# Loads of the first token tiles reordered, norm gains on ScalarE's queue, and two unused products ahead of the first turns, in a hybrid attention and DeltaNet layer

## The reference, cut to what matters

```
hn = _rms_norm(h, norm_gain)
proj = hn @ w_in                      # 1024 -> 3020 columns
(c_q, c_kv, k_idx, w_idx, z_attn, q_g, k_g, v_g, z_g, b_g, a_g) = _split_last(proj, IN_PROJ_SPLITS)
o_attn = _dsa_mixer(c_q, c_kv, k_idx, w_idx, ...) * silu(z_attn)
o_gdn = _gdn_mixer(q_g, k_g, v_g, z_g, b_g, a_g, ...)
y = concatenate([o_attn, o_gdn]) @ w_out
return h + y
```

## Time and profile before

| what | value |
|---|---|
| median of 3 runs | 849.3 us (847.48 to 850.51) |
| profiled execution, its own time | 850.14 us |
| its span, first to last instruction | 848.4 us |
| TensorE busy | 810.3 us, 96% |
| VectorE busy | 605.5 us, 71% |
| ScalarE busy | 390.3 us, 46% |
| GpSimd busy | 252.0 us, 30% |
| mean granted TensorE clock | 0.982 of full |

### The profile page before, as it was taken

The page is one execution under the profiler, slowest core; times in us unless marked ns, Lnnn a source line. Parts: engine busy times, 40 slices in busy tenths (PEclk is TensorE's granted clock), DMA queues, the critical chain, the costliest instruction groups (busy, mean ns, idle before and its releaser), DMA issues.

```text
span 848.4 us, 16491 instructions
## 1 busy us (share of the span) xinstructions
PE 810.3 (96%) x6345; PEld 486.9 (57%) x6345; DVE 605.5 (71%) x1405; ACT 390.3 (46%) x1218; POOL 252.0 (30%) x254
## 2 busy tenths in 40 slices
PE   6999999999999999999969999999899999999998
PEld 2555434444445666666636667766676566566564
DVE  2353789999999999999866667667656665575541
ACT  3444767776692545555445445575421222132111
POOL 8000100000000545467744522355323232332310
PEclk9999999999999999999979999999969999999999
DMA  6262200013003002000100021203221320222011
GB/s 163 83 214 98 77 13 26 25 41 130 30 13 124 0 1 99 1 0 1 46 29 2 25 100 33 85 26 115 95 99 59 101 96 12 96 77 76 27 51 50
DMA packets 29507, 51.72 MB, mean 61 GB/s; under 512 B 3684, under 2 KB 11220, under 8 KB 29428
## 3 DMA queue, kind: packets, MB, share of 16 engines
q1 hardware_dynamic: 28884, 50.55, 17.7%
q0 software_dynamic: 544, 0.10, 0.4%
HBM read 40.11 MB, written 12.10 MB: 62 GB/s over the span
## 4 chain that ended last, share of the span: by engine, by line
PE 87%; DVE 6%; ACT 3%; issue 3%; DMA 1%; POOL 0%; DVEq 0%; ACTq 0%; POOLq 0%
PE ps L1683 20%; PE ps L1661 12%; PE ps L1894 11%; PE ps L1538 7%; PE ps L1732 5%; PE ps L1721 5%; PE ps L1703 4%; PE ps L1795 2%; PE ps L1635 2%; PE ps L1815 2%; PE ps L1856 1%; PE ps L1589 1%; PE ps L1831 1%; PE ps L1870 1%; PE ps L1633 1%
## 5 line engine op out<-in xcount | busy, mean ns | idle before, releaser
L1200 DVE TENSOR_SCALAR_CACHE_REDUCE junk<-scores,iw 128x272 bf16<-128x272 f32 (+6 forms) x224 | 213.6, 954 | 8.2
L1683 PE MATMUL ps<-areaH,areaW 128*128 128x384 f32 (+1 forms) x576 | 168.1, 455 | 1.6 <-ACT areaQ L936 1.6
L1683 PEld LDWEIGHTS ps<-areaH,areaW 128*128 128x128 f32 x576 | 109.4, 190 | 59.9 <-issue 1.8
L748 POOL TENSOR_TENSOR staging<-staging,areaC 128x520 f32<-128x520 f32 x60 | 88.1, 1502 | 63.9 <-ACT areaC L974 63.9
L762 POOL TENSOR_TENSOR areaH<-areaQ,masks 128x512 f32<-128x512 f32 x37 | 45.3, 1229 | 90.1 <-PE ps L1815 82.2
L795 POOL TENSOR_TENSOR areaW<-scores,tmp 128x256 f32<-128x256 f32 (+1 forms) x64 | 45.0, 727 | 62.4 <-DVE small L1286 53.1
L1538 PE MATMUL ps<-areaW,areaH 128*128 128x460 f32 (+1 forms) x144 | 59.9, 571 | 2.0 <-DVE areaH L1122 1.9
L1894 PE MATMUL ps<-areaW,scores 128*128 128x512 f32 x128 | 59.2, 604 | 0.0
L974 ACT ACTIVATE areaC<-areaC,small 128x520 f32<-128x520 f32 x60 | 42.6, 726 | 33.9 <-POOL staging L748 33.9
L1661 PE MATMUL ps<-areaH,areaW 128*128 128x512 f32 x128 | 56.5, 594 | 0.0
L1661 PE MATMUL ps<-areaW,areaH 128*128 128x512 f32 x128 | 56.2, 592 | 0.0
(11 more groups left out here) (272 smaller groups left out, 1439.8 us busy)
## 6 DMA issues: line engine op xcount, KB each, us to landing
areaW<-in_w_in SPq DMA_DIRECT2D x5, 2048.0 KB, 8.0
areaH<-row_factor_scratch SPq DMA_DIRECT2D x18, 256.0 KB, 4.5
areaC<-in_x SPq DMA_DIRECT2D x8, 512.0 KB, 3.6
tmp<-in_x SPq DMA_DIRECT2D x8, 512.0 KB, 5.0
y<-tmp SPq DMA_DIRECT2D x7, 512.0 KB, 3.3
areaW<-in_w_out SPq DMA_DIRECT2D x3, 768.0 KB, 6.6
gate_a_scratch<-staging SPq DMA_DIRECT2D x8, 256.0 KB, 2.3
gate_g_scratch<-staging SPq DMA_DIRECT2D x8, 256.0 KB, 2.0
```

Source lines behind the costliest of these rows:

```text
L748: nc.gpsimd.tensor_tensor(sums, sums, prod, ALU.add).then_inc(s_cvP, 1)
L1200: tlink(V.tensor_scalar(junk[:, 0:n], scores[:, SC0[i]:SC0[i] + n], at, init, op, ALU.add, accum_out=cnt[:, i - 1:i]))
L1683: ins = mm(ps[:, n % 4, 0:hi - lo], wslot[:, g % 2, k, 128 * m:128 * m + 128], hT[:, k, lo:hi], start=k == 0, stop=k == KD - 1)
```

## The change

Three edits at the start of the program:

1. SP waits until the last of the first weights (`w_first7`) has landed before it asks for tiles 2 to 8. Tile 2 was asked for directly behind the issue of those weights.
2. The three loads of gains (`norm_gain` as 128x8 single values, `cq_norm_gain` as 128x2, `ckv_norm_gain` as 128x1) go out from ScalarE's queue, ahead of its table load, and no longer from POOL's.
3. VectorE clears 512 columns of `areaQ` as its third constant (the clearing of `junk` becomes its fourth), and TensorE multiplies that with itself twice into bank 7, a 128x128 by 128x512 f32 product each, ahead of its wait for the identity matrix. Nothing reads the result.

```
-        N_CONST, N_DCONST, N_PAR = 22, 3, 16 * 12
+        N_CONST, N_DCONST, N_PAR = 22, 4, 16 * 12
...
                 if k == 3:
                     load_x(1)
+            sp.wait_ge(s_wk[KD - 1], 16)
             for t in range(2, NT):
                 load_x(t)
...
         @block.gpsimd
         def _(pool):
             par = [
-                (gain, norm_gain[0].rearrange("(k p) -> p k", p=128)),
-                (gc[:, 0:2], g_cq[0].rearrange("(k p) -> p k", p=128)),
-                (gc[:, 2:3], g_ckv[0].rearrange("(k p) -> p k", p=128)),
...
-            for dst, src in par[0:3]:
-                pool.dma_start(dst, src).then_inc(s_gain, 16)
...
-            for dst, src in par[3:]:
+            for dst, src in par:
                 pool.dma_start(dst, src).then_inc(s_par, 16)
...
+            act.dma_start(gain, norm_gain[0].rearrange("(k p) -> p k", p=128)).then_inc(s_gain, 16)
+            act.dma_start(gc[:, 0:2], g_cq[0].rearrange("(k p) -> p k", p=128)).then_inc(s_gain, 16)
+            act.dma_start(gc[:, 2:3], g_ckv[0].rearrange("(k p) -> p k", p=128)).then_inc(s_gain, 16)
             nc.scalar.preload_act_table_set("natural_log_exp_and_others")
             act.wait_ge(s_dconst, N_DCONST)
...
             dlink(V.memset(ba, 0.0))
+            dlink(V.memset(areaQ[:, 0:512], 0.0))
             dlink(V.memset(junk[:, :], 0.0))
...
             mm, turn = nc.tensor.matmul, nc.tensor.transpose
+            pe.wait_ge(s_dconst, 3)
+            for _ in range(2):
+                mm(ps[:, 7, :], areaQ[:, 0:128], areaQ[:, 0:512], start=True, stop=True)
             pe.wait_ge(s_const, 3)
```

## The result

The changed kernel is slower: median 856.4 us of 8 runs (850.56 to 858.12) against 848.39 of 8 runs of the kernel before (845.77 to 850.51) beside them; the ratio is 1.0079, with a 95% interval of 1.0058 to 1.0101. The prediction said 852.7, slower. Its direction was right; its size, +3.4 us, is half of the +6.7 that the ratio gives.

What follows compares the result with a forecast made beforehand. TensorE, busy 96% of the span, was taken as the bound, with projection 1's start deciding. Terms +1.6 + 0.5 + 1.3 + 0 + 0 = +3.4 us on 849.3 gave 852.7 us, range 849.2 to 855.0.

Steps and rivals of the forecast that it cites:

- The number to watch: Start of projection 1 on TensorE, 19.67 us before the change; whatever moves it was to move the rest of the kernel.
- Two chains that end together: Before projection 1, TensorE's own chain and tile 2's arrive at 18.3 within 0.1 us; speeding projection 0 alone gives next to nothing.
- Part 1: SP's wait: weights land at 13.4, tile 2 at 17.3 instead of 15.7; +1.6 us, ends +0.8 and +3.2.
- Part 2: Gains on ScalarE's queue: projection 0 starts near 7.5 instead of 8.61, 1.1 us gained but hidden behind tile 2's chain.
- Part 3: The two products on TensorE, done by 5.3 before turn 0, delay nothing; worth 0 on the path.
- The clock: TensorE idles 4.8 us before turn 2, so its clock falls: +0.5 us in turn 2, +1.3 in projection 1.
- B: Weights land at about 11.8 without tile 2 beside them, cancelling its lateness: -1 to +0.8 us; chance 0.15.
- C: Weights' stream brakes both chains: `w_first7` lands by about 9.3, projection 1 starts at 17.2, -2.5 us; chance 0.08.
- A: Tile 2 is late but TensorE's clock holds or falls briefly: +0.8 to +2.5 us; chance 0.27, shared with another rival.

Runs made afterwards that it cites:

- no_wait: The changed kernel without SP's wait, gains on ScalarE's queue and the two products kept; ratio 1.0050 to the kernel before.
- gains_only: The kernel before with only the gains' loads moved to ScalarE's queue, so POOL's twelve small loads start at 2.10 us instead of 4.97; ratio 1.0068.
- products_only: The kernel before with only the two unused products and the clearing they read; ratio 1.0003.
- wait_only: The kernel before with only SP's wait for the last first weights; ratio 1.0032.
- small_loads_last: The kernel before with POOL's twelve small loads moved behind its last constant and the landing of the last first weights; ratio 0.9998.
- changed_again: The changed kernel unaltered, profiled a second time; 855.92 us, span 854.2.
- broadcast_last: The kernel before with gains on ScalarE's queue and, of POOL's small loads, only that of `gdn_norm_gain` moved behind the last first weights; ratio 1.0036.

## Why the prediction was wrong where it was, point by point

**The number to watch** was nearly right. In eleven kernels beside the one before the time followed the end of projection 1, nearly within what the timing can tell. The start alone is not enough where the low clock follows: in no_wait and gains_only it moved by 2.2 and 2.9 us, and the ratio's interval begins at 2.4 and 3.2.

**Two chains that end together, tile 2's being the one that counts**: right. In products_only the other chain is 1.2 us sooner, whatever made it so, and that gives nothing.

**Part 1, the wait, +1.6 with the weights at 13.4 and an upper bound of 15.0**: this is the step that failed. "I take 13.4, unchanged, as neither end has the better row" was wrong, and so was the bound. The weights landed at 16.2, 17.3 and 16.8. Tile 2's square started 4.0 to 5.1 us later than before instead of 1.6. From landing to square it took 3.6, as reckoned (3.9). Where the weights do land near 13, in wait_only, the term is right: projection 1 +1.8. So it was a mis-sized term and not a wrong mechanism. With 16.2 in place of 13.4 the sum gives 4.4 + 1.8 = +6.2 us, against +6.7 by the ratio.

What I had missed is the small loads. I named them, put their shift at 2.3 us (it was 2.9, from 4.97 to 2.10) and let them cost at most two thirds of it. They cost 2.8 us and more: with all twelve early the weights land at 15.7 to 17.3, with them held or last at 11.3 to 12.3. Could the trace of before have told? Its transfers between 9 and 16 us, by queue (packets, MB, share of 16 engines):

```profile
q1 hardware_dynamic: 693, 1.41, 53.8%
q0 software_dynamic: 439, 0.10, 36.5%
```

POOL's queue, q0, carried 0.10 MB in 36.5% of the engines' time, 0.365 x 7 = 2.6 us of every engine. That should have warned me, but it isn't the price. The run small_loads_last shows that about 1.1 us of it was already paid in the landing at 13.4. The whole of it in front of the weights gives 12.3 + 2.6 = 14.9, and in the changed kernel they landed 1.3 to 2.4 us later still. In the changed kernel q0 takes less of the same stretch, 28.7%, and the weights are later. What the small loads do to the stream beyond their own packets' time stays open.

**Part 2, the gains**: ScalarE's three issues took 0.47, 0.60 and 0.49 us instead of 0.43 each, so its first square started at 3.75 instead of the 3.4 reckoned, and turn 0 at 6.45 (6.1). The gains landed near 5, as by the row of small pieces, and projection 0 started at 7.40 (7.5). Right, and hidden as said. What moves up on POOL's queue behind the removed issues, which I had put under part 1, is its real price, 1.0068 by itself.

**Part 3, the products**: done at 5.27 (5.3), nothing delayed, worth nothing on the path: right. That they bring the full clock sooner came true only in part: turn 0 ran in 0.63 or 0.64 us in four of the seven profiles with them and in 1.00 in the other three, and projection 0 was back at the low clock from 8.2 to 11.6 us in the changed kernel. Projection 0 was to be done by 15.5; it was done at 17.1, held by its last weights, again the failed step.

**The clock, +0.5 and +1.3**: the fall came in all three profiles, in two of them at turn 2 and projection 1, where it cost 0.5 and 1.6 us of projection 1 and doubled turn 2; in changed_again it was low from before 15.2 until 18.5 instead, stretched projection 0, and projection 1 ran at full pace. At the head it cost 1.4 us, 2.5 us and, in changed_again, nothing that counts, against 1.8 in the sum. So the mechanism was right, its size about what the sum had, and it does not strike at the same place each time. Nor does the idle time alone decide it: after 2.7 us without work turn 2 and projection 1 of gains_only ran partly at the low clock, those of wait_only, after 2.7 us as well, did not.

**The rivals.** B and C needed earlier weights. B's reason, tile 2 out of the stream, is tested by wait_only: the weights land at 13.0, 0.4 us sooner and within the scatter, and not at 11.8. They do come near 11.8 (11.3 to 12.3) where the small loads are held or go last; C's 9.3 came nowhere. A's price, wait without the clock, is wait_only: +1.8 at projection 1. That the time lay above the range's 855.0 goes back to the landing behind 15.0: with it at 16.2 the sum comes to 855.5. The forecast's own lower end had a slip of 0.1: 0.8 + 1.3 is 2.1 and not 2.2.

**What stays open**: by what means the small loads hold the weights, which of the eight beside the taps do it, and how the loss (6.7 us by the ratio, 4.9 to 8.6 by its interval) is shared between the head and the clock behind 100 us in the average execution. Three profiles are too few for that.

## What to carry to other kernels

When an edit takes instructions off a queue, price what moves up behind them, transfers above all. A transfer's bytes don't give that price: 0.10 MB took more than a third of the DMA engines' time. That share doesn't give it either: in broadcast_last the taps held the weights back where their queue took 12.9%. What gave it here was a run with the loads held to their old time and one with them last. Loads that nobody needs soon belong behind those that the first product waits for; here that, with the second and third edit and without the wait on SP, was the better kernel, by 0.2%. And one profile of a kernel whose runs spread by 7 us says little about the total; compare the stage that the edit touches.

## What the runs showed that I had not expected

The four tap loads, 6 KB each, issued near 7 us instead of 9.3, held a stream of 1.8 MB back: with them last, the last weights landed at 14.0 instead of 15.7. The effect of POOL's loads hangs on when they start: at 2.1 us the weights land at 15.7, at 5.6 us at 12.0, nearly as early as with all twelve last (11.3 to 12.3). And runs of one and the same kernel, the one before, went from 843.8 us at a granted clock of 0.989 to 851.3 at 0.982, as much as the whole change.
